# RWKV mixing stage: scaling moved to ScalarE, strips reordered, key norms for all tiles at once

## What is computed (reference, cut)

```python
rw = concat([_seq_shift_mix(rw[:, :n_ctx], mu[0], mu[1]), _grid_shift_mix(rw[:, n_ctx:], mu)], axis=1)
# _seq_shift_mix:  z + mu_prev * (prev - z) + mu_next * (nxt - z)
# _grid_shift_mix: g + mu[0]*(left-g) + mu[1]*(right-g) + mu[2]*(up-g) + mu[3]*(down-g)
r, k, v, wd_f, wd_b, ad_f, ad_b, gd_r = _split(rw, ...)      # tanh(wd), sigmoid(gd_r) are used later
kk = k * rwkv_kk.reshape(4, 64)
kk = kk / maximum(sqrt(sum(kk * kk, -1, keepdims=True)), 1e-12)
y  = unboth(_rwkv7_scan(both(r, r), both(w_f, w_b), both(k_f, k_b), both(v, v), both(kk, kk), both(a_f, a_b)))
```

## Time and profile before

| | us |
|---|---|
| median of 3 runs | 5107.22 (5101.8 to 5116.49) |
| the profiled execution, whole | 5059.33 |
| its span, first to last instruction | 5057.5 |
| the mixing stage, from its gate to the next | 2950.92 to about 3029.0 |
| the keys stage, to the scan's first weight load | 3029.07 to 3057.66 |
| mean granted clock of TensorE | 0.911 |

### The profile page before, as it was taken

One profiled execution on the slowest core, in us unless ns is written; L12 is line 12 of the kernel. 1 busy time (PEld: TensorE's weight loads), 2 busy tenths in 40 slices (PEclk: granted clock), 3 DMA queues, 4 the chain that ended last, 5 costly groups with the idle time before them and its releaser, 6 DMA issues. The chain is left out here.

```text
span 5057.5 us, 68248 instructions
## 1 busy us (share of the span) xinstructions
PE 4293.7 (85%) x27634; PEld 2406.0 (48%) x27634; DVE 1984.6 (39%) x4148; ACT 1360.4 (27%) x3110; POOL 520.9 (10%) x564
## 2 busy tenths in 40 slices
PE   6998799999997999999987626787688899999992
PEld 2454466644444665444456515676235343333331
DVE  1631556613515663321026576665345111111115
ACT  2111545511115553111024333332032111111110
POOL 0000000000000000000000001221003322222220
PEclk8999889999998999999988857988798899999996
DMA  4011000120210004311110030000303688889884
GB/s 184 21 62 67 5 14 14 71 84 27 64 65 5 14 14 163 117 51 67 67 61 2 2 97 2 3 3 2 108 0 125 263 259 275 276 296 337 303 262 131
DMA packets 147952, 503.23 MB, mean 100 GB/s; under 512 B 22721, under 2 KB 71474, under 8 KB 134194
## 3 DMA queue, kind: packets, MB, share of 16 engines
q1 hardware_dynamic: 110338, 377.80, 20.0%
q0 software_dynamic: 37296, 120.99, 9.1%
HBM read 402.42 MB, written 96.32 MB: 99 GB/s over the span
## 5 line engine op out<-in xcount | busy, mean ns | idle before, releaser
L697 PE MATMUL banks<-arena 128*128 128x512 f32 (+1 forms) x2928 | 1108.2, 540 | 16.5 <-DMA arena<-in_w_in 10.8
L697 PEld LDWEIGHTS banks<-arena 128*128 128x128 f32 x2928 | 559.0, 191 | 564.0 <-issue 522.8
L3100 PE MATMUL banks<-arena 128*32 128x512 f32 (+2 forms) x2896 | 560.5, 594 | 3.1 <-DMA arena<-in_experts 2.3
L884 PE MATMUL banks<-arena 128*128 128x512 f32 (+1 forms) x896 | 373.5, 571 | 23.4 <-DMA arena<-y_d 17.7
L1248 PE MATMUL banks<-arena 96*128 96x512 f32 (+1 forms) x800 | 376.9, 554 | 11.7 <-ACT arena L1351 10.0
L3100 PEld LDWEIGHTS banks<-arena 128*32 128x32 f32 (+2 forms) x2896 | 197.8, 130 | 356.9 <-issue 354.2
L1298 DVE TENSOR_REDUCE arena<-banks 128x1 f32<-128x512 f32 (+1 forms) x400 | 238.1, 595 | 242.6 <-PE banks L1248 241.1
L3120 PE MATMUL banks<-arena 128*32 128x512 f32 (+2 forms) x1448 | 296.3, 615 | 1.3 <-ACT arena L3178 1.3
L884 PEld LDWEIGHTS banks<-arena 128*128 128x128 f32 x896 | 171.6, 193 | 218.6 <-issue 213.3
L3067 POOL DMA_INDIRECT r_d<-arena x125 | 181.4, 1451 | 702.5 <-DMA r_d<-arena 278.3
L3157 DVE SCALAR_TENSOR_TENSOR arena<-arena,banks 128x256 f32<-128x256 f32 x79 | 38.1, 482 | 533.9 <-ACT arena L3192 533.9
(11 more groups left out here) (507 smaller groups left out, 5658.4 us busy)
## 6 DMA issues: line engine op xcount, KB each, us to landing
arena<-in_experts SPq DMA_DIRECT2D x64, 3072.0 KB, 12.9
arena<-in_ada_w SPq DMA_DIRECT2D x12, 2048.0 KB, 7.6
arena<-in_w_in SPq DMA_DIRECT2D x19, 1024.0 KB, 5.7
arena<-in_w_mod SPq DMA_DIRECT2D x8, 2048.0 KB, 17.9
arena<-in_w_in SPq DMA_DIRECT2D x7, 2048.0 KB, 8.9
arena<-in_w_out SPq DMA_DIRECT2D x6, 2048.0 KB, 10.6
arena<-in_w_mod SPq DMA_DIRECT2D x8, 1024.0 KB, 5.2
u<-arena POOLq DMA_DIRECT2D x28, 256.0 KB, 2.3
```

The lines of the kernel that those rows point to most:

```text
L697: i = e.matmul(self.out_of(n), lhs, rhs, start=k == 0, stop=k == KT - 1)
L884: i = e.matmul(bank(n % 4)[:, 0:nn], w[:, q, :], H[:, q, t0:t0 + nn], start=q == 0, stop=q == KT - 1)
L3100: op = e.matmul(ABK[(q - q0) % 2][rows, :], xT[(q - q0) % 2][:, P * k:P * k + P][:, rows], weights[:, i % SLOTS, 512 * k:512 * k + 512], s ...
```

## The change

Mixing: all nine strips get a buffer of their own (`inr`), and their loads are issued ahead of the row broadcasts and the weights, with no wait. The strips are taken in the order 2, 3, 6, 7, 8, 0, 1, 4, 5 (k, k, the three low-rank strips, r, r, v, v), with three `outr` buffers. The scaling by the own factor is two ScalarE activations (Copy with a per-partition scale) for each strip, three strips ahead of VectorE. VectorE keeps the six additions; the context's and the grid's are issued in pairs between waits, so that three waits on itself are left in a strip. BS and Y are cleared by VectorE before the first strip.

Keys: no stage of its own any more. After the sixth strip VectorE multiplies K by the `rwkv_kk` row for all ten tiles in one instruction (128x2560); ScalarE squares it in one; after the eighth strip VectorE sums into 128x40; ScalarE takes the roots; after the ninth strip VectorE takes maximum and reciprocal and multiplies, again in one instruction of 128x2560. `begin` and its wait are gone.

```diff
--- before.py
+++ after.py
@@ -2040,27 +2040,37 @@
         w2, a2, g2 = al(256), al(256), al(256)
         cc_ = al(18)
         mark = al.o
-        inr, outr = [al(1280), al(1280)], [al(1280), al(1280)]
+        inr, outr = [al(1280) for _ in range(9)], [al(1280) for _ in range(3)]
+        sq, norms = al(2560), al(40)
         b4 = lambda a: a.unsqueeze(2).broadcast_to([P, 4, 64])
         mix = "rwkv"
+        sources = [2, 3, 6, 7, 8, 0, 1, 4, 5]
+        turned = [i for i in sources if i < 6]
+        mixed = lambda i: outr[turned.index(i) % 3] if i < 6 else lo_[i - 6]
+        heads = lambda a: a.rearrange("p (g n) -> p g n", n=64)
 
         def mix_sync(e):
             Tn, Vn, Sn, Gn = points(mix)
+
+            def source(i):
+                ld.turn(e)
+                e.dma_start(inr[i], B["rw_d"][P * i:P * i + P, :]).then_inc(ld.hit(mix, "in", i), 16)
+
+            for i in sources[0:3]:
+                source(i)
             srcs = [A["rwkv_w0_2"][0, 0], A["rwkv_a0_2"][0, 0], A["rwkv_w0_2"][0, 1], A["rwkv_a0_2"][0, 1], A["rwkv_kk_2"][0], A["rwkv_ka_2"][0],
                     A["rwkv_rk_2"][0].rearrange("a b -> (a b)"), A["rwkv_lnx_w_2"][0], A["rwkv_lnx_b_2"][0]]
+            for i in sources[3:]:
+                source(i)
             for i, src in enumerate(srcs):
                 row_bcast(e, rb[i], src, mix, "row", i)
             for nm, dst, src in (("w2", w2, A["rwkv_w2_2"][0].rearrange("a k n -> (a k) n")), ("a2", a2, A["rwkv_a2_2"][0].rearrange("a k n -> (a k) n")),
                                  ("g2", g2, A["rwkv_g2_2"][0])):
                 ld.turn(e)
                 e.dma_start(dst, src).then_inc(ld.hit(mix, nm), 16)
-            for i in range(9):
-                if i >= 2:
-                    e.wait_ge(*Vn.at("mix", i - 2))
-                ld.turn(e)
-                e.dma_start(inr[i % 2], B["rw_d"][P * i:P * i + P, :]).then_inc(ld.hit(mix, "in", i), 16)
 
         def mix_vector(e):
+
             Tn, Vn, Sn, Gn = points(mix)
             mu = lambda j: col("mu", 9 * j, 9)
             e.tensor_tensor(cc_[:, 0:9], mu(0), mu(1), ALU.add).then_inc(Vn.hit(), 1)
@@ -2069,57 +2079,86 @@
             e.wait_ge(*Vn.own())
             e.tensor_tensor(cc_[:, 9:18], cc_[:, 0:9], mu(2), ALU.subtract).then_inc(Vn.hit(), 1)
             e.wait_ge(*Vn.own())
-            e.tensor_tensor(cc_[:, 9:18], cc_[:, 9:18], mu(3), ALU.subtract).then_inc(Vn.hit(), 1)
-            e.wait_ge(*Vn.own())
-            for i in range(9):
-                a, o_ = inr[i % 2], outr[i % 2] if i < 6 else lo_[i - 6]
+            e.tensor_tensor(cc_[:, 9:18], cc_[:, 9:18], mu(3), ALU.subtract).then_inc(Vn.hit("own"), 1)
+            e.memset(BS, 0.0).then_inc(Vn.hit(), 1)
+            e.memset(Y, 0.0).then_inc(Vn.hit(), 1)
+            for n, i in enumerate(sources):
+                a, o_ = inr[i], mixed(i)
                 mc = [reg(cols["mu"] + 9 * j + i, 1) for j in range(4)]
                 og, ag = (v[:, NCTX:T].rearrange("p (r c) -> p r c", c=GRIDW) for v in (o_, a))
-                e.wait_ge(*ld.at(mix, "in", i))
-                if 2 <= i < 6:
-                    e.wait_ge(*Tn.at("turned", i - 2))
-                e.tensor_scalar(o_[:, 0:NCTX], a[:, 0:NCTX], cc_[:, i:i + 1], None, ALU.mult).then_inc(Vn.hit(), 1)
-                e.tensor_scalar(o_[:, NCTX:T], a[:, NCTX:T], cc_[:, 9 + i:10 + i], None, ALU.mult).then_inc(Vn.hit(), 1)
-                e.wait_ge(*Vn.own())
+                e.wait_ge(*Sn.at("own", i))
                 e.scalar_tensor_tensor(o_[:, 1:NCTX], a[:, 0:NCTX - 1], mc[0], o_[:, 1:NCTX], ALU.mult, ALU.add).then_inc(Vn.hit(), 1)
+                e.scalar_tensor_tensor(og[:, :, 1:GRIDW], ag[:, :, 0:GRIDW - 1], mc[0], og[:, :, 1:GRIDW], ALU.mult, ALU.add).then_inc(Vn.hit(), 1)
                 e.wait_ge(*Vn.own())
                 e.scalar_tensor_tensor(o_[:, 0:NCTX - 1], a[:, 1:NCTX], mc[1], o_[:, 0:NCTX - 1], ALU.mult, ALU.add).then_inc(Vn.hit(), 1)
-                e.wait_ge(*Vn.own())
-                e.scalar_tensor_tensor(og[:, :, 1:GRIDW], ag[:, :, 0:GRIDW - 1], mc[0], og[:, :, 1:GRIDW], ALU.mult, ALU.add).then_inc(Vn.hit(), 1)
-                e.wait_ge(*Vn.own())
                 e.scalar_tensor_tensor(og[:, :, 0:GRIDW - 1], ag[:, :, 1:GRIDW], mc[1], og[:, :, 0:GRIDW - 1], ALU.mult, ALU.add).then_inc(Vn.hit(), 1)
                 e.wait_ge(*Vn.own())
                 e.scalar_tensor_tensor(o_[:, NCTX + GRIDW:T], a[:, NCTX:T - GRIDW], mc[2], o_[:, NCTX + GRIDW:T], ALU.mult, ALU.add).then_inc(Vn.hit(), 1)
                 e.wait_ge(*Vn.own())
                 e.scalar_tensor_tensor(o_[:, NCTX:T - GRIDW], a[:, NCTX + GRIDW:T], mc[3], o_[:, NCTX:T - GRIDW], ALU.mult, ALU.add).then_inc(Vn.hit("mix", i), 1)
+                if n == 5:
+                    e.wait_ge(*ld.at(mix, "row", 4))
+                    e.wait_ge(*Sn.at("rows", 5))
+                    e.tensor_tensor(KK, K, rb[4].unsqueeze(1).broadcast_to([P, NT, 256]), ALU.mult).then_inc(Vn.hit("kk"), 1)
+                if n == 7:
+                    e.wait_ge(*Sn.at("sq"))
+                    e.tensor_reduce(norms, heads(sq), AX.X, ALU.add).then_inc(Vn.hit("sum"), 1)
+            e.wait_ge(*Sn.at("root"))
+            e.tensor_scalar(norms, norms, 1e-12, None, ALU.max).then_inc(Vn.hit(), 1)
+            e.wait_ge(*Vn.own())
+            e.reciprocal(norms, norms).then_inc(Vn.hit(), 1)
+            kkh = KK.rearrange("p j n -> p (j n)")
+            e.wait_ge(*Vn.own())
+            e.tensor_tensor(heads(kkh), heads(kkh), norms.unsqueeze(2).broadcast_to([P, 40, 64]), ALU.mult).then_inc(Vn.hit(), 1)
 
         groups4 = [(t0, min(4, NT - t0)) for t0 in range(0, NT, 4)]
 
         def mix_tensor(e):
             Tn, Vn, Sn, Gn = points(mix)
-            for i in range(6):
+            for n, i in enumerate(turned):
                 e.wait_ge(*Vn.at("mix", i))
-                for q, (t0, n) in enumerate(groups4):
-                    u = 3 * i + q
+                for q, (t0, w_) in enumerate(groups4):
+                    u = 3 * n + q
                     if u >= 2:
                         e.wait_ge(*Sn.at("rows", u - 2))
-                    for j in range(n):
-                        op = e.transpose(bank(6 + u % 2)[:, P * j:P * j + P], outr[i % 2][:, P * (t0 + j):P * (t0 + j) + P], ident)
+                    for j in range(w_):
+                        op = e.transpose(bank(6 + u % 2)[:, P * j:P * j + P], mixed(i)[:, P * (t0 + j):P * (t0 + j) + P], ident)
                     op.then_inc(Tn.hit("rows", u), 1)
                 Tn.note("turned", i)
 
         def mix_scalar(e):
             Tn, Vn, Sn, Gn = points(mix)
-            for i in range(6):
-                dst, c0 = (R, K, V)[i // 2], P * (i % 2)
-                for q, (t0, n) in enumerate(groups4):
-                    u = 3 * i + q
-                    e.wait_ge(*Tn.at("rows", u))
-                    e.activation(dst[:, t0:t0 + n, c0:c0 + P], bank(6 + u % 2)[:, 0:P * n].rearrange("p (j n) -> p j n", j=n), ACT.Copy).then_inc(Sn.hit("rows", u), 1)
-            e.wait_ge(*Vn.at("mix", 6))
-            e.activation(lo_[0], lo_[0], ACT.Tanh).then_inc(Sn.hit(), 1)
-            e.wait_ge(*Vn.at("mix", 8))
-            e.activation(lo_[2], lo_[2], ACT.Sigmoid).then_inc(Sn.hit(), 1)
+
+            def own(i):
+                a, o_ = inr[i], mixed(i)
+                e.wait_ge(*ld.at(mix, "in", i))
+                if i < 6 and turned.index(i) >= 3:
+                    e.wait_ge(*Tn.at("turned", turned[turned.index(i) - 3]))
+                e.activation(o_[:, 0:NCTX], a[:, 0:NCTX], ACT.Copy, scale=cc_[:, i:i + 1]).then_inc(Sn.hit(), 1)
+                e.activation(o_[:, NCTX:T], a[:, NCTX:T], ACT.Copy, scale=cc_[:, 9 + i:10 + i]).then_inc(Sn.hit("own", i), 1)
+
+            e.wait_ge(*Vn.at("own"))
+            for i in sources[0:3]:
+                own(i)
+            for n, i in enumerate(sources):
+                if i < 6:
+                    dst, c0 = (R, K, V)[i // 2], P * (i % 2)
+                    for q, (t0, w_) in enumerate(groups4):
+                        u = 3 * turned.index(i) + q
+                        e.wait_ge(*Tn.at("rows", u))
+                        e.activation(dst[:, t0:t0 + w_, c0:c0 + P], bank(6 + u % 2)[:, 0:P * w_].rearrange("p (j n) -> p j n", j=w_), ACT.Copy).then_inc(Sn.hit("rows", u), 1)
+                else:
+                    e.wait_ge(*Vn.at("mix", i))
+                    if i != 7:
+                        e.activation(lo_[i - 6], lo_[i - 6], ACT.Tanh if i == 6 else ACT.Sigmoid).then_inc(Sn.hit(), 1)
+                if n + 3 < 9:
+                    own(sources[n + 3])
+                if n == 6:
+                    e.wait_ge(*Vn.at("kk"))
+                    e.activation(sq, KK.rearrange("p j n -> p (j n)"), ACT.Square).then_inc(Sn.hit("sq"), 1)
+                if n == 7:
+                    e.wait_ge(*Vn.at("sum"))
+                    e.activation(norms, norms, ACT.Sqrt).then_inc(Sn.hit("root"), 1)
 
```

(32 more changed lines are left out.)

## The result

| | before | after |
|---|---|---|
| median of four runs, us | 5106.67 (5101.8 to 5116.49) | 5056.99 (5051.64 to 5070.24) |
| ratio | | 0.9905, 95% interval 0.9886 to 0.9924 |
| the profiled execution | 5059.33 | 5051.64 |
| its span | 5057.5 | 5049.7 |
| gate to the scan's first weight load | 106.7 | 66.7 |

The kernel is 50 us faster by its median (39 to 58 by the interval), where 40 were forecast. The spans of the two profiled executions differ by only 7.8 us, though. The stages say why. A stage is measured from the first instruction or load behind its gate to that of the next. The changed part lost 40.0 us; the routing stage, 800 us behind it and untouched by the change, took 45.6 us longer; the experts' stage took 11.8 less and the scan 1.7.

What follows compares the result with a forecast made beforehand. VectorE's chain between the gate and the scan, 106.7 us, was taken as the bound. Savings of 7.3 (head), 11.7 (strips) and 21 (keys) make 40 us off the median 5107.2, giving 5067.2 us, range 5050 to 5088.

Steps and rivals of the forecast that it cites:

- The head: From the gate to VectorE's first addition: the first strip's load, issued first, lands sooner; 7.3 us saved.
- The strips: Nine mixing strips on VectorE: scaling leaves and three additions stop waiting; 5.79 us each against 7.09, 11.7 saved.
- The big instructions: Keys: 2.81 us for each 128x2560 VectorE product or sum, about 0.4 for the reciprocal, 2.34 for ScalarE's square.
- The part: Mixing and keys, from the gate to the scan's first weight load: 66.7 us, not 106.7.
- The bound for strips that arrive together: Head rival: strips share the load engines, so the first comes 7 us later (+7.3); with dear instructions, chance 0.10.
- wait at the gate for moved loads: Rival at the gate: moved loads arrive late; forecast said they are there after some 25 us, 40 ahead of it.
- the 21 us of the keys: Keys saving: from the last addition's end to the scan, 30.0 us before against 9.
- The table load: Keys: the root's load, 1.28 us by the row, gets cover; by the skill's 2.66 the saving would be 1.4 larger.
- ScalarE as the place for a multiplication: Strip scaling: 1.55 us on ScalarE against 1.05 on VectorE, but on an idle engine, so the sum doesn't take it.
- ScalarE becomes the bound: Strips rival: scaling takes 3.1 us, a turned strip 6.2; about 5 us less saved, 5072; chance 0.04.
- the stage goes at that pace: 0.4 x 9: Strips, if scaling takes 3.1 us: nine strips each 0.4 us slower, plus 1.55 at the start, about 5 less saved.
- More than the sum: Scan's first 23 us: TensorE's clock may rise earlier, at most some 5 us more saved, 5062; chance 0.06.

Runs made afterwards that it cites:

- after_third: The changed kernel executed again with no edit, beside the kernel before: changed part 66.8 us, median 5011.5 us, ratio 0.9903 to the kernel before.
- rows_first: The changed kernel with row broadcasts and three weights issued ahead of the nine strips, as before: part 75.6 us, 8.7 more; median 5019.76 us.
- vector_scales: The changed kernel with VectorE scaling the strips itself, as before: part 74.5 us, 7.6 more; ratio 0.9948 to the kernel before.
- waits_back: The changed kernel with VectorE waiting for itself ahead of every addition again, in the new order: part 68.9 us, 2.0 more.
- key_tiles: The changed kernel with the keys in ten tiles in their own stage, as before: part 87.1 us, 20.2 more; ratio 0.9959 to the kernel before.
- double_scale: The changed kernel with ScalarE scaling each strip twice, once into a buffer nobody reads: part 68.2 us, 1.3 more.

## Why the prediction was right, and where it was not

- **The head.** Forecast: landing 3.9 us after issue, first addition 5.5 behind the gate. Measured 4.0 and 5.6. That the queue serves strips in the order of issue, some 1.6 us apart, was read from two landings of before and held. In after_third, issue to landing, all nine strips and then the first two alone:

```profile
DMA to landing us min/median/max: 4.0/8.1/13.1
...
DMA to landing us min/median/max: 4.0/4.6/5.2
```

The first two were issued 0.4 us apart, the first and the last 4.0: so the second landed 1.6 us behind the first, and the last 13.1 behind it, 1.64 for a strip. rows_first shows the same from the other side.

- **The strips.** Forecast 5.79 from start to start; measured 5.79. Splitting the 11.7 us by the runs: 9.4 for the scaling (vector_scales), 2.0 to 2.2 for the waits (waits_back).
- **The big instructions.** Forecast 2.81 for 128x2560, 0.43 for the reciprocal, 2.34 for the square; measured 2.81 and 2.82, 0.40 and 2.33. The slope between the sums of 256 and 768 elements carried over to 2560. The square's price was a row of that very size. For the reciprocal one row of 256 was at hand, and no working leads from it to 0.4: that it came out right is partly luck.
- **The part.** Forecast 66.7 us, measured 66.7. The bound for strips that arrive together did not come up; nor did any wait at the gate for moved loads (the last was issued at 2965.93). Where the 21 us of the keys come from is shown by key_tiles only as a whole (20.2).
- **The table load.** "ScalarE: Activation LUTs", What ACT_TABLE_LOAD costs, in the Trainium skill counts 2.66 us with its drain. The root's load took 1.28, straight behind a copy, and its activation starts 1.30 behind the load's start (3008.82 to 3010.12); no drain shows in this trace.
- **ScalarE as the place for a multiplication.** Rules for kernel authors, on the same page of the Trainium skill, speaks for VectorE, with bf16 as its example; for a strip's scaling in fp32 the trace agrees: 1.54 us from start to start on ScalarE (2955.17 to 2956.71) against 1.04. The part is shorter by 7.6 us with ScalarE all the same, as that engine is idle there.
- **A rival's price that was wrong.** "ScalarE becomes the bound" was put at some 5 us lost if scaling took 3.1 us. double_scale has just that, and lost 1.3, all of it in the first strip. The step that failed is "the stage goes at that pace: 0.4 x 9". The pace itself, 3.1 + 3.1, was too slow: the first 3.1 us hold TensorE's transposes ahead of the first copy, and ScalarE was scaling meanwhile (5.71 us for a strip, 0.89 of them idle). Besides, only six strips are turned, and the lead of three strips, which the prediction names, is not in this sum.
- **The term that was missing.** The sum took the scan as unchanged. It is 3.8 us shorter in two later sessions (1.7 in the first), with a higher granted clock in its first 100 us. "More than the sum" names the clock and has up to 5 us, but its mechanism is not what happened: in the scan's first 23 us the clock was 0.50 before and 0.52 after, at or next to the lower of its two levels (1.2 GHz), so it hardly rises earlier; the difference comes later in the first 100 us. What sets it is open. It was equal in each repeat of a program in the later sessions (0.77 twice for before, 0.82 twice for after) but not in the first (0.85 and 0.87), 0.82 with key_tiles, though TensorE idles ahead of its scan there as it did before, and 0.77 with rows_first, which turns strips up to the gate. So neither the idle time ahead of the scan nor its absence explains it.
- **The absolute time.** 5067.2 was forecast and 5056.99 measured, 10 us lower: 1.7 are the scan's in that session. The remaining 8 lie within what four runs of each can tell (39 to 58 us saved); the later sessions, with 45 us between the kernels, leave 1 unexplained. Taking the saving off the runs' median and not off the profiled execution came out right for that session, but without its reason: nothing in the trace before told that the kernel after would be slow by the same 45 to 50 us. The forecast for the profiled execution, 5019, was missed by 33 us: the 45.6 of the routing stage, less what the experts' stage and the scan gave (11.8 and 1.7).

## What to carry to other kernels

Where one engine carries a stage, count its instructions' start-to-start distances from the trace and move to an idle engine what that one can do well ahead, even if it takes it half as long again; with a lead of three strips, even twice the price there cost 1.3 us here. Before moving work to GpSimd, ask whether VectorE's instructions beside it read two operands from SBUF, since here a product of 5.57 us stopped VectorE for 5.2. And when a profile pair disagrees with the medians, set the lengths of all stages side by side before explaining anything in the one that was changed.

## What the hardware showed unexpectedly

- A store issued by SyncE was seen as landed 68 us later, while GpSimd issued indirect scatters without a break; in the twelve other profiles of the same code the stage took 166.4 to 166.9 us, not 212.1. What decides between the two forms wasn't tried, and the scatters run beside the stores in the short form too.
- An addition of VectorE that began 0.17 us after a product of GpSimd took 6.42 us instead of 1.22.
- TensorE's granted clock in the first 100 us of the same scan was 0.77 to 0.88 in thirteen profiles. In the later sessions it differed from program to program and was the same each time for the two programs that were repeated; in the first session both had more (0.85 and 0.87). The scans beside it took 538 to 526 us.
